# ScalarE's order in three attentions, and the low parts of four covered norms moved to VectorE

## What is computed

```python
def modulate(x, norm_w, shift, scale):
    return rms_norm(x, norm_w) * (1 + scale) + shift
def one_block(qblk):                       # latent attention, 128 queries at a time
    s = jnp.einsum('bqhd,bkhd->bhqk', qblk, k) * scale
    return jnp.einsum('bhqk,bkhd->bqhd', jax.nn.softmax(s, axis=-1), v)
...
out = rms_norm_2(out, subln_g) * (1.0 - lam_init)      # per head of the differential attention
y = concatenate([ya, yb], -1);  return (y * jax.nn.silu(g)) @ w_out
...
y = acc * e[..., None] / (l * e + jnp.exp(sk - M))[..., None]     # banded attention with sinks
return (y * jax.nn.silu(g)) @ w_out
```

## Time and profile before

| | us |
|---|---|
| median of 3 runs | 2313.79 (2313.37 to 2314.4) |
| the profiled execution | 2312.39 |
| its span in the trace | 2310.4 |
| TensorE busy | 2234.4 (97%) |
| TensorE's weight loads (beside its products) | 1910.9 |
| VectorE busy | 1190.9 (52%) |
| ScalarE busy | 881.2 (38%) |
| GpSimd busy | 939.4 (41%) |

### The profile page before, as it was taken

The page is one execution under the profiler, slowest core; times in us unless marked ns, Lnnn a source line. Parts: engine busy times, 40 slices in busy tenths (PEclk is TensorE's granted clock), DMA queues, the critical chain, the costliest instruction groups (busy, mean ns, idle before and its releaser), DMA issues.

```text
span 2310.4 us, 36915 instructions
## 1 busy us (share of the span) xinstructions
PE 2234.4 (97%) x13959; PEld 1910.9 (83%) x13959; DVE 1190.9 (52%) x1929; ACT 881.2 (38%) x1536; POOL 939.4 (41%) x764
## 2 busy tenths in 40 slices
PE   6999999999999999999999999999999999899998
PEld 4878979888888888888889887778887887688777
DVE  4684771657777763425243355663333106761273
ACT  5434343341111122335446442223443236652562
POOL 2435453343433333334433255565755440154303
PEclk9999999999999999999999999999999999999999
DMA  7232241126555531112110035552223321123212
GB/s 280 73 147 74 69 161 60 58 97 207 187 189 190 183 135 64 59 60 94 50 42 19 28 109 185 188 182 93 98 91 98 100 91 65 58 80 95 69 47 73
DMA packets 67721, 245.40 MB, mean 106 GB/s; under 512 B 7377, under 2 KB 11729, under 8 KB 66961
## 3 DMA queue, kind: packets, MB, share of 16 engines
q1 hardware_dynamic: 67360, 242.94, 30.9%
q0 software_dynamic: 240, 0.79, 0.1%
HBM read 240.81 MB, written 2.10 MB: 105 GB/s over the span
## 4 chain that ended last, share of the span: by engine, by line
PE 67%; issue 9%; DVE 3%; POOL 3%; ACT 2%; POOLq 0%; DVEq 0%; ACTq 0%
PE ps L870 13%; PE ps L871 12%; PE ps L872 12%; PE ps L1755 4%; PE ps L1758 4%; PE ps L1757 4%; POOL w_low L486 3%; PE ps L1923 1%; PE ps L633 1%; PE ps L907 1%; PE ps L908 1%; PE ps L909 1%; PE ps L1971 1%; PE ps L1985 1%; DVE arena L687 1%
## 5 line engine op out<-in xcount | busy, mean ns | idle before, releaser
L486 POOL TENSOR_TENSOR w_low<-ring,w_high 128x512 fp32r<-128x512 f32 (+2 forms) x534 | 755.8, 1437 | 1093.6 <-ACT w_high L477 1093.6
L477 ACT ACTIVATE w_high<-ring 128x1024 fp32r<-128x1024 f32 (+2 forms) x267 | 274.8, 1031 | 925.2 <-PE ps L872 626.2
L870 PE MATMUL ps<-h_high,w_high 128*128 128x512 f32 x1040 | 412.2, 396 | 11.7 <-POOL w_low L486 8.4
L871 PE MATMUL ps<-h_low,w_high 128*128 128x512 f32 x1040 | 408.4, 393 | 0.0
L872 PE MATMUL ps<-h_high,w_low 128*128 128x512 f32 x1040 | 407.7, 392 | 0.0
L870 PEld LDWEIGHTS ps<-h_high,w_high 128*128 128x128 f32 x1040 | 197.1, 189 | 63.2 <-POOL w_low L486 10.6
L872 PEld LDWEIGHTS ps<-h_high,w_low 128*128 128x128 f32 x1040 | 197.0, 189 | 42.0
L871 PEld LDWEIGHTS ps<-h_low,w_high 128*128 128x128 f32 x1040 | 197.2, 190 | 38.4
L3199 DVE TENSOR_TENSOR hidden<-arena,hidden 128x1536 fp32r<-128x1536 f32 (+1 forms) x42 | 87.2, 2076 | 193.3 <-ACT hidden L2339 193.3
L1755 PE MATMUL ps<-hidden,w_high 128*128 128x512 f32 (+1 forms) x504 | 178.6, 354 | 0.0
L1757 PE MATMUL ps<-hidden,w_high 128*128 128x512 f32 (+1 forms) x504 | 178.5, 354 | 0.0
(11 more groups left out here) (547 smaller groups left out, 4776.9 us busy)
## 6 DMA issues: line engine op xcount, KB each, us to landing
const<-late_w_dram SPq DMA_DIRECT2D x112, 512.0 KB, 4.9
ring<-up_dram SPq DMA_DIRECT2D x88, 512.0 KB, 3.3
ring<-down_dram SPq DMA_DIRECT2D x44, 512.0 KB, 3.2
XB<-ada_dram SPq DMA_DIRECT2D x22, 768.0 KB, 5.6
ring<-winE_dram SPq DMA_DIRECT2D x32, 512.0 KB, 3.5
ring<-win_dram SPq DMA_DIRECT2D x20, 512.0 KB, 3.2
ring<-winC_dram SPq DMA_DIRECT2D x20, 512.0 KB, 3.5
arena<-ada_dram SPq DMA_DIRECT2D x10, 768.0 KB, 19.8
```

The lines of the kernel that those rows point to most:

```text
L477: nc.scalar.activation(WH[p][:, 0:L], RAW[p][:, 0:L], ACT.Copy).then_inc(w_hi, 1)
L486: ins = nc.gpsimd.tensor_tensor(WL[p][:, to], RAW[p][:, to], WH[p][:, to].bitcast(F32), ALU.subtract)
L870: nc.tensor.matmul(bank[:, 0:n], wh[:, cols], hi, start=(k == 0), stop=False)
L871: nc.tensor.matmul(bank[:, 0:n], wh[:, cols], lo, start=False, stop=False)
```

## The change

1. **Covered norms** (n2 to n5, their first segment). All eight low parts are made on VectorE by `even_low`, each two tiles behind its scaling; line 720's extra activation and GpSimd's `odd_low` are gone there. The copy of the row comes after all low parts and now frees the spread sum's bank; tile 7's scaling has a semaphore of its own. ScalarE rounds weight chunk 2 ahead of all tiles and chunk 3 between tiles 6 and 7. GpSimd has only the weights' low parts left.
2. **Latent attention.** On ScalarE the copy of u-2 comes before the Exp of u, and the first key parts (5, 6) behind the four copies of the "fa" sums.
3. **E and C attentions.** On ScalarE, in the first steps (s < 4), the copy of s-2 comes before the Exps of s. Weight chunks 0 and 1 of woutE and woutC are rounded at s = 6 and s = 10 and no longer before the attention. After E, the root comes ahead of the rounding of woutE's chunk 2.
4. **y of C.** ScalarE rounds pair p at s = 9 + 4p, and only pair 7 after the attention. The low parts of pairs 0 to 6 are on GpSimd, behind w_low of woutC's chunks 0 and 1; VectorE makes only that of pair 7. Pairs 0 to 3 have their low parts in a new place (`y_low_first`).

```diff
@@ shift_high, even_low, parted norms (ScalarE, VectorE, GpSimd) @@
-                if j % 2:
+                if j % 2 and not (stage in DEFERRED and k == 0):
                     ins = nc.scalar.activation(dsts[j], dsts[j], ACT.Identity, bias=shifts[j])
...
+            if stage in DEFERRED and k == 0:
+                for j in range(KT + 3):
+                    if j < KT:
+                        scale_tile(stage, k, j)
+                    if 2 <= j < KT + 2:
+                        even_low(stage, k, j - 2)
+                row_copy(stage)
+                return
...
-            for j in range(1, KT, 2):
+            for j in () if stage in DEFERRED and k == 0 else range(1, KT, 2):
                 odd_low(stage, k, j)
@@ deferred_shift (ScalarE) @@
-                shift_high(norm, 0, range(2))
                 split_hi(stage, 2, 0, (stage, 0, 0))
-                shift_high(norm, 0, range(2, KT))
+                shift_high(norm, 0, range(KT - 1))
                 split_hi(stage, 3, 0, (stage, 1, 0))
+                shift_high(norm, 0, (KT - 1,))
@@ E and C attention (ScalarE) @@
+                    if s < 4:
+                        turned_first(*units[s - 2])
                     if s < n:
                         exponentials(*units[s])
+                    if s in (6, 10):
+                        split_hi("woutC" if kinds == ("c",) else "woutE", (s - 6) // 4)
...
-                    turned_first(*units[s - 2])
+                    if s >= 4:
+                        turned_first(*units[s - 2])
+                    if kinds == ("c",) and s >= 9 and s % 4 == 1:
+                        pair_high((s - 9) // 4)
...
-            split_hi("woutE", 0)
-            split_hi("woutE", 1)
-
             attention("a", "b")
             load_table(ROOT)
             for h in range(2, 4):
                 diff_square(h)
-            split_hi("woutE", 2)
             act.wait_ge(diff_summed, 4)
             A(DIFF_ROOTS, DIFF_ROOTS, ACT.Sqrt, bias=small[:, 0:1], scale=1.0 / P).then_inc(diff_rooted, 1)
+            split_hi("woutE", 2)
...
-            split_hi("woutC", 0)
-            split_hi("woutC", 1)
             attention("c")
-            await_taken(act, *spread_inverse("c", 7))
-            y_high(HL, YH, S)
+            pair_high(7)
@@ GpSimd, stage woutC @@
+                    for k in range(KT - 1):
+                        pool.wait_ge(y_hi, 24 + k + 1)
+                        TT(pair_low(k), HL[:, k, :], YH[:, k, :].bitcast(F32), ALU.subtract).then_inc(c_low, 1)
@@ VectorE @@
-            y_low(HL, YH, YLo, S, 24)
+            y_low(HL, YH, YLo, S, 24, (KT - 1,))
```

More of the change, by code:

```diff
@@ L784, in row_copy @@
         def row_copy(norm):
-            nc.vector.tensor_copy(ROW, bank_ap(*spread_sum(norm, 0))).then_inc(u_row, 1)
+            taken(nc.vector.tensor_copy(ROW, bank_ap(*spread_sum(norm, 0))), *spread_sum(norm, 0))
         def unscaled_sums(pe, norm, x, between):
@@ L923, in h_there, with there @@
         def h_there(pe, norm):
-            return lambda s, k: pe.wait_ge(h_odd if k % 2 else h_even, (KT // 2) * (PARTED[norm] + s) + k // 2 + 1)
+            def there(s, k):
+                if norm in DEFERRED and s == 0:
+                    pe.wait_ge(h_last, KT * list(DEFERRED).index(norm) + k + 1)
+                else:
+                    pe.wait_ge(h_odd if k % 2 else h_even, (KT // 2) * (PARTED[norm] - COVERED_BEFORE[norm] + s) + k // 2 + 1)
+            return there
         def in_part(x, s, k, low_):
@@ L2152, in _ @@
             shift_high("n0", 1)
-            def y_high(y, to, n):
-                for k in range(KT):
-                    A(to[:, k, :], y[:, k, 0:n], ACT.Copy).then_inc(y_hi, 1)
             def hgrn(r):
@@ L2522, in _ @@
                     split_hi("woutM", u - 5)
+                if u >= 2:
+                    w = u - 2
+                    if w >= 3:
+                        h, i = divmod(w - 3, 4)
+                        if i == 3:
+                            await_sums(act, "mV", h)
+                        else:
+                            act.wait_ge(m_val, 3 * h + i + 1)
+                    await_sums(act, "mT", w)
+                    taken(A(M_T[:, w % 3, :, :], ps[:, 4:6, :].rearrange("p b n -> p (b n)")[:, 0:T]
+                            .rearrange("p (t n) -> p t n", t=6), ACT.Copy), "mT", w)
                 if u < 24:
@@ L2810, in _ @@
                         TT(YLo[:, k, :], HL[:, k, :], YH[:, k, :].bitcast(F32), ALU.subtract).then_inc(y_first, 1)
+                if stage == "woutC":
+                    first = 1
+                    for k in range(2):
+                        split_lo(stage, k)
+                    for k in range(KT - 1):
+                        pool.wait_ge(y_hi, 24 + k + 1)
+                        TT(pair_low(k), HL[:, k, :], YH[:, k, :].bitcast(F32), ALU.subtract).then_inc(c_low, 1)
                 with pool.Fori(first, n // 2) as i:
```

54 lines of the change are left out of this document (27 added, 27 removed).

## The result

The changed kernel takes 2292.32 us (median, 2290.17 to 2296.84) beside 2313.58 (2310.37 to 2314.4): a ratio of 0.9913, 95% interval 0.9896 to 0.9931, so 16 to 24 us less. Run again later it took 2294.72 beside 2313.45, ratio 0.9913 (0.9898 to 0.9928). Forecast were 2297.0, in a range of 2288.5 to 2305.5.

A forecast was written before the change was run, and what follows sets the result against it. TensorE, busy 2234.4 of 2310.4 us, was taken as the bound, so only its waits and clock count. Terms -2.7 - 2.6 - 4.4 - 3.7 - 3.9 + 0.5 = -16.8 took 2313.8 to 2297.0 us, range 2288.5 to 2305.5.

The forecast's parts named there:

- Latent attention: Two TensorE waits for ScalarE's copy go, -2.4, and moved key parts save about 0.3: -2.7 us.
- Start of E: TensorE's wait of 2.59 us for a copy goes whole, and roundings at steps 6 and 10 cost nothing: -2.6 us.
- end of E: With the root first TensorE resumes 3.0 us earlier, plus 1.4 of half clock: -4.4, bounds 3.0 and 5.5.
- end of C: Seven pairs of y ready early; wait -2.3 and half clock -1.6: -3.9 us, bounds 2.3 and 4.
- Start of C: First norms 4.3 us earlier, 0.6 given back for roundings at steps 6 and 10: -3.7, bounds 2.5 and 5.
- n2: Covered norm: last low part ends about 13 us after the first scaling, chunk 3 starts when it did: 0.
- n3: Covered norm: late high part 0, taps and Silus delay chunk 4's w_low: +1.9 to +2.8, taken as +2.5 us.
- n4: Covered norm: chunk 2 rounded before any tile, chunk 3 starts near 1745 instead of about 1747.5: -2.5 us.
- n5: Covered norm: high part 0 2.2 us later, chunk 3 starts at the last low part's end: 0 to +0.9, taken +0.5.
- the first: Rival: the covered norms gain too, -7 in place of +0.5, giving 2289.5 us; chance 0.18.
- The second: Rival: the norms cost 3, the clock isn't had back, attentions give idle time alone, 13.1: 2303.5 us; chance 0.22.
- The slower case: Rival: covered norms' low parts on VectorE cost 1.78 each beside GpSimd, +26 us, giving 2323 us; chance 0.05.

The follow-up runs named there:

- wc_behind: The changed kernel with woutE's and woutC's roundings at steps 6 and 10 put behind the turned unit's copy: 2291.58 us.
- order_only: The kernel before with only the order of ScalarE's weight roundings in the covered norms changed, odd low parts still on GpSimd: 2314.9 us beside 2312.45, ratio 1.0019.
- norms_only: The kernel before with only the covered norms' part of the change: 2312.79 us beside 2312.45, ratio 0.9991.
- up4_early: The changed kernel with the rounding of up1's chunk 4 ahead of the Silus in n3: 2292.92 us beside 2312.45 for the kernel before.
- root_first: The kernel before with the root ahead of the rounding of woutE's third chunk: 2307.86 us beside 2311.39, ratio 0.9982.

## Right or wrong, step by step

- **What bounds it.** Right: nearly all gains are at TensorE's waits and at the clock behind them; winM's 1.5 has no wait ahead of it. (That no other engine has half as much to do was a slip: VectorE is busy 52%.) Of the first pair's 22.2 us of span, TensorE's idle time gives 9.3 (76.0 to 66.7) and its busy time 12.9; 1.1 of the first and 2.6 of the second lie ahead of n2 and are chance. Behind it that leaves 8.2 of idle time and 10.3 of clock, so over half of the gain is clock, where the sum had 4.1 of 16.8. The sum came within 1 us partly by luck: idle time was taken too high and the clock too low.
- **Latent attention**, -2.7 against -3.3. The two waits of 1.2 went with a little more each; the moved key parts gave their upper bound, 0.5. No Exp was late for TensorE.
- **Start of E, end of E, end of C**, -2.6, -4.4, -3.9 against -2.8, -4.6, -3.9. Right in place and size, and in the start of E and the end of C in the parts too. At the end of E two errors cancel: idle time fell by 1.6 where I had 3.0 (1.2 us of waits are left), and the half clock went whole, worth 3.0, where I had 1.4. The root did start at the place named, 2006.0 on the old time scale. In E's steps 6 and 10 the roundings cost 0.4 where I had nothing.
- **Start of C**, -3.7 against -2.9. The first step was right (-4.4, I had 4.3); what failed is the 0.6 for the roundings in steps 6 and 10, which cost 1.5. I compared the rounding with ScalarE's idle time in a step, but it was put ahead of the very copy that TensorE waited for next. `wc_behind` shows it. Waits behind steps 6 and 10 were among my signs of being wrong, and they came. The rounding of y's pairs cost nothing that can be seen, as said.
- **n2**, 0 against -1.6, and 1.5 more at winM. I took chunk 3's start as set by the last low part with collisions; in fact only the first low part was held up by w_low (1.42 us). The last three took 2.06 together although w_low of chunk 3 started beside them: GpSimd's piece was the one that waited. Why it waits in n2 and n4 and VectorE in n3 and n5 isn't shown. Whether winM's missing half-clock stretch belongs to n2 is open: the three traces with n2's old timing, and `order_only`, whose n2 ends 0.4 later, have two stretches there (between 1148 and 1175); of the eight with the new timing seven have one, and `wc_behind` has three times that.
- **n3**, +2.5 against +4.1. The mechanism was right to the row: idle VectorE, eight low parts, late taps, Silus, chunk 4. (The 0.6 for a low part that meets w_low was too little for the last two, which took 1.0 more each.) Chunk 4 started 2.3 us late, inside the +1.9 to +2.8. What failed is the clock: I read chunk 4's time before with half clock behind chunk 3's wait in it, and didn't count the like stretch that my own longer wait brings behind chunk 4, 1.7 us.
- **n4**, -2.5 against -2.5: the number is right by luck. I expected the last low part to end near 1744.3 and chunk 3 to start right behind it, near 1745, and left the half clock open. On the old time scale the last low part ended at 1742.6, 1.7 earlier, since GpSimd paid for the collision. Chunk 3 started at 1745.05 all the same, behind a wait of 1.37 for the w_low that had been held up. TensorE's idle time in n4 fell by 0.2 alone: the old wait of 2.53 came back as 1.1 for low parts and 1.4 for w_low. The gain is the half-clock stretch of 6.8 us that went.
- **n5**, +0.5 against +0.7. Right: the last low part ended at 2076.8, inside the 2076.2 to 2076.9.
- **Rivals.** The norms gained nothing on the whole (`norms_only`), so the first fell; by the lock's time alone, 2.4 us a norm, the norms should have gained, but what counted was the order in which low parts and the roundings came. The second fell too: the clock was had back. Waits were exchanged in the norms (3.0 us less for w_low, 5.6 more for low parts), and little in the attentions. The slower case needed low parts of 1.5 us on the mean; they took 0.74 (n4), 0.82 (n2) and 1.11 (n3, n5), though the last two of n3 and of n5 reached the 1.8 that I had named as a bad sign.

## To carry to other kernels

Where one engine is busy 97% of the time, look only at what it waits for, and at what stands ahead of the releasing instruction in its own engine's list: the attentions' part, nearly all of it instructions moved within ScalarE's list, gave all of the gain, and 16 low parts moved between engines gave none until the roundings around them were put in order. (At the end of C seven low parts went to GpSimd as well; no run separates them from the roundings.) When work is put into an engine's idle time, the place within the step counts more than the length: behind the instruction that the bound engine waits for, never ahead of it. A forecast that hits the time should be checked in its parts too: at the end of E and in n4 it was right by errors that cancel. And gains below 0.2% are seen by laying two traces over each other place by place, not by medians, since single executions of the kernel before ranged from 2306.68 to 2316.99 us.

## What the chip showed that was not expected

- Half clock comes behind waits, but not behind each: after 3.10 us of wait it was granted 0.51 (changed kernel, 1369 to 1372), after 2.36 us it stayed at full clock (`up4_early`, 1371). Nor does it take a wait: in the kernel before no wait of TensorE is seen between 1140 and 1172 us, and the clock was still 0.57 from 1154 to 1158. What stands ahead of it are 24 products of a single column (the row below). The changed kernel has the same row, at 1145.55, and kept full clock behind it. Removing a wait at one place can make half clock appear at a later one that had none: `root_first` won 5.0 us and lost 1.6 at n5; `norms_only` and `order_only` got a new stretch at E's start. But for the last of each trace, such stretches were 3.4, 6.8 or 10.2 us long.
- What a VectorE operation loses beside GpSimd's w_low is no fixed factor: the same low part took 0.74 alone, and 1.12, 1.28, 1.42 or 1.77 where it met one piece of w_low. The Trainium skill ("SBUF — State Buffer", section "SBUF: two separate sides") calls the port pair that the two engines share an exclusive lock, for VectorE with two SBUF inputs. It names also operations in a 2-port performance mode. The low parts agree with the first. For the second there is a tap with one SBUF input: a `TENSOR_SCALAR` that takes 0.55 us from SBUF and 0.80 from PSUM took 1.64 from SBUF beside w_low; in which mode it ran no run here shows.
- Which engine pays isn't told by the recorded starts: in n3 a GpSimd piece starts at 1355.44 and a low part at 1355.56, and the low part takes 1.77; in n2 they start at 1067.64 and 1067.76, as far apart, and the GpSimd piece takes 2.68.
- Ahead of the first change the same kernel's traces differ by up to 4 us, in the first transfer's wait and in where half clock falls before 500 us.

TensorE ahead of the half clock at 1154 us in the kernel before:

```profile
1150.83 2.73 PE L633 MATMUL ps<-const,SQ 128*128 128x1 f32 x24
```
